# Grouped-query mixing with split values as weights, feature-major, and a written table of slots

## The reference

```python
def windowed_gqa_sink(q, k, v, sink):
...
    s = jnp.einsum('bnqhgd,bnkhd->bnhgqk', qb, kb).astype(jnp.float32) * (dh ** -0.5)
    s = jnp.where(mask[None, :, None, None], s, -jnp.inf)
...
    m = jnp.maximum(jnp.max(s, axis=-1, keepdims=True), sink_l)
    e = jnp.exp(s - m)
    p = e / (jnp.sum(e, axis=-1, keepdims=True) + jnp.exp(sink_l - m))
    o = jnp.einsum('bnhgqk,bnkhd->bnqhgd', p.astype(v.dtype), vb)

def second_block(...):
...
        merged = jax.nn.sigmoid(ga) * (ya @ w_branch_a[l]) + jax.nn.sigmoid(gb) * (yb @ w_branch_b[l])
        h = h + merged @ w_out[l]
```

## Time and profile before

| | |
|---|---|
| median of 3 runs | 960.63 us (960.3 to 960.73) |
| the profiled execution | 960.34 us, span of its instructions 958.5 us |
| granted clock | 0.998 |
| PE busy | 951.3 us, 99% |
| DVE busy | 655.8 us, 68% |
| ACT busy | 533.7 us, 56% |

### The profile page before, as it was taken

One profiled execution on the slowest core, in us unless ns is written; L12 is line 12 of the kernel. 1 busy time (PEld: TensorE's weight loads), 2 busy tenths in 40 slices (PEclk: granted clock), 3 DMA queues, 4 the chain that ended last, 5 costly groups with the idle time before them and its releaser, 6 DMA issues.

```text
span 958.5 us, 14072 instructions
## 1 busy us (share of the span) xinstructions
PE 951.3 (99%) x5478; PEld 834.8 (87%) x5478; DVE 655.8 (68%) x842; ACT 533.7 (56%) x692; POOL 57.6 (6%) x92
## 2 busy tenths in 40 slices
PE   9999999999999999999999999999999999999997
PEld 8999988888888888898888888999888898888886
DVE  6778869866665565688666566878656676566665
ACT  7577678436444444474454445678664464444544
POOL 2200000002000000022221000100000020000000
PEclk9999999999999999999999999999999999999999
DMA  9684444553755655547666555644345546665541
GB/s 308 206 255 133 132 132 159 196 181 127 266 192 188 206 175 185 187 155 247 205 214 208 180 184 166 210 141 137 130 132 176 176 167 206 200 194 180 187 160 44
DMA packets 117440, 173.17 MB, mean 181 GB/s; under 512 B 3152, under 2 KB 89440, under 8 KB 117392
## 3 DMA queue, kind: packets, MB, share of 16 engines
q1 hardware_dynamic: 115824, 168.32, 54.2%
q0 software_dynamic: 1424, 3.91, 1.4%
q10 hardware_dynamic: 144, 0.26, 0.1%
HBM read 171.44 MB, written 1.05 MB: 180 GB/s over the span
## 4 chain that ended last, share of the span: by engine, by line
PE 98%; DMA 1%; DVE 0%; SPq 0%; ACT 0%; issue 0%
PE pair L683 22%; PE pair L686 11%; PE acc L665 10%; PE acc L667 10%; PE acc L666 10%; PE pair L665 8%; PE pair L667 8%; PE pair L666 8%; PE acc L1198 1%; PE acc L1041 1%; PE pair L893 1%; PE acc L1184 1%; PE acc L810 1%; DMA raw<-in_w_in 1%; PE acc L876 1%; PE acc L729 0%
## 5 line engine op out<-in xcount | busy, mean ns | idle before, releaser
L683 PE MATMUL pair<-actp,wh 128*128 128x512 f32 x912 | 292.8, 396 | 0.0
L1735 DVE TENSOR_TENSOR wl<-raw,wh 128x2048 fp32r<-128x2048 f32 x89 | 204.9, 2303 | 62.5 <-ACT wh L1301 62.5
L1301 ACT ACTIVATE wh<-raw 128x2048 fp32r<-128x2048 f32 x88 | 168.4, 1913 | 83.5 <-PE acc L667 83.5
L686 PEld LDWEIGHTS pair<-actp,wl 128*128 128x128 f32 x912 | 171.3, 188 | 40.0
L686 PE MATMUL pair<-actp,wl 128*128 128x256 f32 x912 | 179.2, 278 | 0.0
L1730 DVE TENSOR_TENSOR wl<-raw,wh 128x2048 fp32r<-128x2048 f32 x68 | 155.4, 2288 | 31.0 <-ACT wh L1295 30.6
L1295 ACT ACTIVATE wh<-raw 128x2048 fp32r<-128x2048 f32 x69 | 132.1, 1916 | 77.4 <-PE pair L667 54.3
L683 PEld LDWEIGHTS pair<-actp,wh 128*128 128x128 f32 x912 | 141.6, 189 | 1.4
L1514 ACT ACTIVATE arena<-pair 128x512 f32<-128x512 f32 x57 | 34.1, 598 | 170.9 <-PE pair L683 170.9
L665 PE MATMUL acc<-wh,midh 128*128 128x512 f32 x310 | 120.9, 390 | 0.0
L667 PE MATMUL acc<-wh,midl 128*128 128x512 f32 x310 | 120.6, 389 | 0.0
(11 more groups left out here) (348 smaller groups left out, 1380.9 us busy)
## 6 DMA issues: line engine op xcount, KB each, us to landing
raw<-in_w_in SPq DMA_DIRECT2D x37, 1024.0 KB, 5.3
raw<-in_mlp_w SPq DMA_DIRECT2D x32, 1024.0 KB, 5.3
raw<-in_ffn_w_gate SPq DMA_DIRECT2D x22, 1024.0 KB, 5.3
raw<-in_ffn_w_up SPq DMA_DIRECT2D x22, 1024.0 KB, 5.3
raw<-in_ffn_w_down SPq DMA_DIRECT2D x22, 1024.0 KB, 5.0
raw<-in_w_out SPq DMA_DIRECT2D x8, 1024.0 KB, 5.0
raw<-in_w_up_rnn SPq DMA_DIRECT2D x4, 1024.0 KB, 5.2
raw<-in_cmp_k_w SPq DMA_DIRECT2D x2, 1024.0 KB, 5.7
```

Source lines behind the costliest of these rows:

```text
L683: return nc.tensor.matmul(bank[:, :].rearrange("p (u t) -> p u t", u=2), h[:, k, cs], actp[:, :, k, :], **kw)
L686: return nc.tensor.matmul(bank[:, 0:T], l[:, k, cs], acth[:, k, :], **kw)
L1301: nc.scalar.activation(wh[:, n % R, :], raw[:, n % R, :], ACT.Copy).then_inc(hi_ready, 1)
L1735: nc.vector.tensor_tensor(wl[:, n % R, :], raw[:, n % R, :], wh[:, n % R, :].bitcast(F32), ALU.subtract).then_inc(lo_ready, 1)
```

## The change

The neighbourhood heads keep their instructions. For the grouped-query heads (in the diff, the first `heads2` is that of ACT and the second that of DVE):

- The values become f32r weights. `vbs` holds, for each half of the keys and each group, 64 columns of the high part and 64 of the low part side by side, 128 in all. ACT copies the high part (in the round of `QB + 1`), and DVE subtracts the low part; before, one DVE copy filled `vb`.
- The probabilities are divided ahead of the transposes (`scale2`, on DVE), one slot behind the score. They alternate between two buffers, `prob2` and `prob3`.
- The transposed probabilities are split: ACT copies the high part to `pth` (`copy2`), and DVE subtracts the low part to `ptl` (`low_probs`).
- `mix2` multiplies each of the two value blocks with `pth` and `ptl`: four matmuls of 256 columns. The outcome is feature-major: partitions 0 to 63 hold the high values' product, 64 to 127 the low values'.
- ACT moves the lower rows down (`low_rows` into `ylow`), and DVE adds them (`norm2`) into `ybT`, which is feature-major. The two `turn_out` of `btok` are gone; ACT copies and DVE splits `ybT` directly.
- The table `turn2` is replaced by separate slots for score, scale, turn and mix (`SCORE_SLOTS` and the lists beside it). The turn stands two slots behind the score, and for the grouped heads the mix stands one slot behind the turn. The last mix moves from slot 31 to slot 33, right ahead of panel `BR`.

```diff
-        turn2 = {(QKV2 + 2 + k, 1): k for k in range(7)}
-        turn2[QKV2 + 9, 1] = 7
-        turn2[QKV2 + 10, 1] = 8
-        for k in range(9, 17):
-            turn2[QKV2 + 11 + (k - 9) // 2, (k - 9) % 2] = k
-        turn2[QKV2 + 15, 1] = 17
+        SCORE_SLOTS = (5, 7, 9, 11, 13, 15, 17, 19, 21, 22, 23, 25, 26, 27, 29, 30)
+        score_at = places(SCORE_SLOTS)
+        scale_at = places([at + 1 for at in SCORE_SLOTS])
+        turn_at = places((7, 9, 11, 13, 15, 17, 19, 21, 23, 24, 25, 27, 28, 29, 31, 32))
+        mix_at = places((9, 11, 13, 15, 17, 19, 21, 22, 24, 25, 26, 28, 29, 30, 32, 33))
...
             def mix2(k):
+                vt = head2(k)[3]
+                pe.wait_ge(normed, NH + k)
+                if k >= NH:
+
+                    pe.wait_ge(ptl_ready, k - NH + 1)
+                    if k == NH:
+                        pe.wait_ge(vb_ready, 1)
+                    for kt in range(TT):
+                        for pt in (pth, ptl):
+                            m = nc.tensor.matmul(ps[4][:, 0:T], vt[kt], pt[:, kt, :], start=kt == 0 and pt is pth,
+                                                 stop=kt == 1 and pt is ptl)
+                    m.then_inc(mixed, 1)
+                    return
...
-                if n == GB2 + 3:
-                    pe.wait_ge(normed, 3 * NH)
-
-                    pe.wait_ge(midl_ready, 3)
-                    for i in range(2):
-                        turn_out(OUT_B[i], btok, 2 * i)
...
+            def low_rows(k):
+
+                act.wait_ge(mixed, NH + k + 1)
+                act.wait_ge(normed, NH + k)
+                nc.scalar.activation(ylow[0:DH, :], ps[4][DH:2 * DH, 0:T], ACT.Copy).then_inc(ylow_ready, 1)
...
             def heads2(n, part):
+                if mix_at.get((n, part), 0) >= NH:
+                    low_rows(mix_at[n, part])
+                if (n, part) in turn_at:
+                    copy2(turn_at[n, part])
+                if (n, part) in score_at:
+                    exp2(score_at[n, part])
...
+            def scale2(k):
+
+                dve.wait_ge(exped, NH + k + 1)
+                o = k % 3
+                c = coef[:, o, 0:TT]
+                link(nc.vector.tensor_tensor(c, sums[:, o, 0:TT], esink[:, o, :], ALU.add))
+                link(nc.vector.reciprocal(c, c))
+                prob = prob_of(k)
+                for tt in range(TT):
+                    m = nc.vector.tensor_scalar(prob[:, tt, :], prob[:, tt, :], coef[:, o, tt:tt + 1], None, ALU.mult)
+                m.then_inc(scaled, 1)
+
+            def low_probs(k):
+
+                dve.wait_ge(probT_ready, NH + k + 1)
+                nc.vector.tensor_tensor(ptl.rearrange("p k t -> p (k t)"), ps[3][:, :],
+                                        pth.rearrange("p k t -> p (k t)").bitcast(F32), ALU.subtract).then_inc(ptl_ready, 1)
...
             def heads2(n, part):
+                if scale_at.get((n, part), 0) >= NH:
+                    scale2(scale_at[n, part])
+                if (n, part) in score_at:
+                    mask2(score_at[n, part])
+                if turn_at.get((n, part), 0) >= NH:
+                    low_probs(turn_at[n, part])
+                if (n, part) in mix_at:
+                    norm2(mix_at[n, part])
```

More of the change, by code:

```diff
@@ L194, in build @@
         kbT = carve(12288, T)
-        vb = carve(13056, TT, P)
         prob2 = carve(13312, TT, T)
         probT2 = carve(13824, 512)
+        prob3 = carve(13824, TT, T)
+        pth, ptl = mrgl[:, 4:6, :], mrgl[:, 6:8, :]
+        ylow = thr
+        vbs = midh[:, 4:6, :].rearrange("p k t -> p (k t)").rearrange("p (k g s d) -> p k g s d", k=TT, g=GR, s=2)
         atok2 = carve(14336, TT, NH * DH)
-        btok = xs[:, 0, :].rearrange("p (t n) -> p t n", t=TT)
+        ybT = xs[:, 0, :].rearrange("p (k t) -> p k t", t=T)
         vbT = xs[:, 0, 0:T]
@@ L369, in build @@
         qb_ready = sem("qb_ready")
+        vbh_ready = sem("vbh_ready")
         vb_ready = sem("vb_ready")
+        scaled = sem("scaled")
+        ptl_ready = sem("ptl_ready")
+        ylow_ready = sem("ylow_ready")
         out_ready = [sem(f"out_ready{b}") for b in range(2 * TT)]
@@ L633, in head2, with prob_of @@
             return (qst[:, h, :], mrgl[:, g, :], mrgl[:, GR + g, :],
-                    [vb[:, kt, DH * g:DH * (g + 1)] for kt in range(TT)])
+                    [vbs[:, kt, g, :, :].rearrange("p s d -> p (s d)") for kt in range(TT)])
+        def prob_of(k):
+            return prob3 if k >= NH and k % 2 else prob2
         def spread_to(j):
             return ps[TURNED[0]][:, 0:T] if j == 3 else ps[3][:, 0:T]
-        OUT_A, OUT_B = 5, (4, 5)
+        OUT_A = 5
         LOW, HIGH, LAST = (0, 1), (4, 5), (6, 7)
@@ L1202, in heads2 @@
             def heads2(n, part):
[L1203 to L1211, removed]
+                if (n, part) in mix_at:
+                    mix2(mix_at[n, part])
+                if (n, part) in turn_at:
+                    turn2_(turn_at[n, part])
+                if (n, part) in score_at:
+                    score2(score_at[n, part])
             def free_bank2(n):
@@ L1637, in _ @@
                 if n == BR:
+                    heads2(n - 1, 1)
                     done(BR - 1)
                     for i in range(2):
-                        out_hi(acth, i, OUT_B[i], 3 + i + 1)
+                        act.wait_ge(normed, 2 * NH + 4 * i + 4)
+                        nc.scalar.activation(acth[:, 2 * i:2 * i + 2, :], ybT[:, 2 * i:2 * i + 2, :], ACT.Copy).then_inc(midh_ready, 1)
                     gates2(n)
@@ L1683, in _ @@
                     swap(swk, kbT[:, :])
-                heads2(n - 1, 1)
+                if n == QB + 1:
+                    act.wait_ge(vb_turned, 1)
+                    nc.scalar.activation(vbs[:, :, :, 0, :], ps[OUT_A][:, 0:T].rearrange("p (k g d) -> p k g d", k=TT, g=GR),
+                                         ACT.Copy).then_inc(vbh_ready, 1)
+                if n != BR:
+                    heads2(n - 1, 1)
                 heads2(n, 0)
@@ L2196, in norm2 @@
                 dve.wait_ge(mixed, NH + k + 1)
                 o = k % 3
-                h = k % NH
                 c = coef[:, o, 0:TT]
[L2200 to L2205, removed]
+                link(nc.vector.reciprocal(c, sums[:, o, 0:TT]))
```

72 lines of the change are left out of this document (41 added, 31 removed).

## The result

The changed kernel takes **965.78 us** (median of 6 runs, 965.08 to 966.63) against 960.49 (960.02 to 960.73) beside it: ratio 1.0057 [1.0046, 1.0068]. The forecast was 962.9, range 960.0 to 965.3: slower, as forecast, but by more than the range held. The profiled execution takes 965.23, its span is 963.2.

What follows compares the result with a forecast made beforehand. PE was taken as the bound, 99% busy with one wait; new waits of 5.77 us less 3.5 spared gave +2.3, so 962.9 us. Its own range was 961.4 to 964.6, widened to 960.0 to 965.3.

Steps and rivals of the forecast that it cites:

- What PE was spared: On PE: cheaper mixes for eight heads and no `btok` transposes, about -3.5 us if nothing waits.
- The prediction's own two terms, 2.8 and 0.88: On PE: new mix 0.35 less a head, 2.8 for eight; eight `btok` transposes with their transition gone, 0.88.
- The division's multiply: On DVE in `scale2`, 256 columns: taken as 0.27 to the next; nearest row 0.409, estimate from the page 0.29.
- Where the waits stand: PE waits for DVE in slots 24, 25, 28, 29 and 32, summing to 5.77 us, none behind `BR`.
- the waits stay out: Rival: PE gets no waits and keeps its 3.5 us, time 957.1; 12%.
- the chains are a little shorter: Rival: each chain link 0.1 less, two long waits lose 1.4 each, -0.5 in all, 960.1; 13%.
- How long the chain is: ACT and DVE links from panel `QKV2 + 12`'s end to slot 28's mix: 688.59 to 702.51, wait 1.79.
- the clock falls: Rival: new PE waits bring half speed for one panel, 5.5 us more, 968.4; 7%.

Runs made afterwards that it cites:

- e9_gates_later: Changed kernel with panel-end `low_rows` and copy ahead of `hi`, and three rounds' gates a round later, behind the next slot's head work: 958.41 us, 0.9982.
- e6_low_first: Changed kernel with copies ahead of `hi`, gates a round later, `lo` held back in three rounds, slot 27's `low_probs` ahead of division and mask: 961.17 us, 1.0005.
- e2_gates_late: Changed kernel with only the gates of rounds 11, 13 and 15 a round later on ACT, behind the copy and exponentials: 960.66 us, 1.0003.
- after_again: The changed kernel itself, unaltered, run and traced again for the spread of its times: 966.83 us (5 runs), 1.0059.

## Why the prediction was half right

The median lies 2.9 above the forecast. About 0.9 of it is the chains, taken too short, less some saving that was taken too small; about 2.0 is the clock, which the sum had at nothing.

**What PE was spared: right.** Old instructions gone, new ones in: forecast 3.5. From slot 21 to `BR` the kernel before takes 50.59. The changed one without a fall takes 53.81, of which 6.64 are waits by the starts and 0.45 five restarts of 0.09 (a mix behind a wait takes 0.55 to 0.58 to its follower, else 0.47): 46.72 of work, 3.9 less and so a little more than forecast. `e9_gates_later` gives 48.49 - 1.40 - 0.27 = 46.82, or 3.8. The prediction's own two terms, 2.8 and 0.88, already make 3.7 and not 3.5. The mix costs 0.47 for the 0.48 forecast. Two groups of new instructions in the changed kernel (busy us, mean ns, idle before):

```profile
L1217 PE MATMUL acc<-mrgl,midh 128*128 128x256 f32 x32 | 5.5, 295 | 5.8 <-DVE mrgl L2250 4.9 <-issue 0.6 <-DVE xs L2257 0.2
...
L2244 DVE TENSOR_SCALAR arena<-arena,coef 128x256 f32<-128x256 f32 x16 | 4.9, 351 | 0.3
```

The division's multiply is 351 ns, on the line through 128 and 512 columns, and not 409. From 128 to 256 and to 512 columns it grows by 0.53 and 0.51 ns a column, and DVE's subtractions of 512 and 2048 columns (0.69 and 2.28 us) by 1.04. In this the trace agrees with the Trainium skill's doubled rate for it (VectorE: DVE Perf Modes, "The perf-mode tier table"), though not with the 0.29 that I estimated from the page.

**Where the waits stand: right.** Slots 24, 25, 28, 29 and 32, and none elsewhere from slot 21 on in this trace. From the starts they are 0.80, 0.26, 2.53, 0.34 and 2.65, plus 0.09 each: 7.0 where 5.8 was forecast (7.1 in the trace without a fall). The rivals *the waits stay out* and *the chains are a little shorter* fall.

**How long the chain is: the term that was mis-sized.** The chain to slot 28 was put at 13.9 us from the panel's end to PE. Its instructions in the changed kernel, ACT and then DVE:

```profile
688.49 1.91 ACT L1315 ACTIVATE wh<-raw 128x2048 fp32r<-128x2048 f32 x1 [2.22 <-PE pair L681]
690.43 0.38 ACT L1612 ACTIVATE thr<-acc 64x256 f32<-64x256 f32 x1
690.83 0.60 ACT L1606 ACTIVATE mrgl<-acc 128x512 fp32r<-128x512 f32 x1
...
696.69 0.48 ACT L1626 ACTIVATE esink<-small,nmax 128x1 f32<-128x1 f32 x2 [2.44 <-DVE nmax L1847]
...
698.18 0.60 ACT L1644 ACTIVATE midh<-acc 128x512 fp32r<-128x512 f32 x1
698.68 1.26 ACT L1660 ACTIVATE arena<-pair,hrstd 128x512 f32<-128x512 f32 x2
699.82 1.92 ACT L1315 ACTIVATE wh<-raw 128x2048 fp32r<-128x2048 f32 x1
701.62 0.61 ACT L1606 ACTIVATE mrgl<-acc 128x512 fp32r<-128x512 f32 x1
```

```profile
691.47 0.69 DVE L2250 TENSOR_TENSOR mrgl<-acc,mrgl 128x512 fp32r<-128x512 f32 x1 [0.38 <-ACT mrgl L1606]
692.19 0.42 DVE L2257 TENSOR_TENSOR xs<-acc,thr 64x256 f32<-64x256 f32 x1
692.64 2.29 DVE L1764 TENSOR_TENSOR wl<-raw,wh 128x2048 fp32r<-128x2048 f32 x1
694.85 0.15 DVE L2240 TENSOR_TENSOR coef<-sums,esink 128x2 f32<-128x2 f32 x1
...
695.77 0.48 DVE L1847 CUSTOM_DVE_ANT_0 arena<-acc,cst,small 128x256 f32<-128x256 f32 x1
...
702.26 0.69 DVE L2250 TENSOR_TENSOR mrgl<-acc,mrgl 128x512 fp32r<-128x512 f32 x1 [1.02 <-ACT mrgl L1606]
```

The order is the forecast's, link for link, and the length 14.6 (688.49 to 703.10). Many links were right: division 0.92 for 0.93, gates 1.14, the second `hi` 1.80. Six were taken too short. Five were put at a distance at which the next instruction starts some 0.1 us before the last one's end, as the copy at 701.62 does behind `hi` (699.82 and 1.92), and here it starts only behind that end; the sixth is the hand-over to PE. They are `hi` ahead of `low_rows` 1.94 for 1.81, `low_rows` 0.40 for 0.30, the low part ahead of the sum 0.72 for 0.61, the sum 0.45 for 0.34, the exponentials ahead of `out_hi` 1.49 for 1.37, the low part to PE 0.84 for 0.72. Together they are the 0.7 that was missing (the other links sum to what was forecast); in the second chain 0.4 were. What decides whether two instructions of an engine overlap so (both kinds wait for semaphores here) stays open, and no run tried it.

**The clock: the step that failed.** The sum took PE's matmuls at full clock behind every wait, and the rival *the clock falls* had 7% and 5.5 us, for a whole panel at half speed; the range left it out. In 10 of 12 runs it falls, once or twice by the levels of time, and takes 1.6 each time, since it is full again within some 3.5 us. Where it does not fall the kernel takes 963.4 to 963.6, inside the range in spite of the chains: it is the falls that carried the median out of it. By its own words ("its one idle stretch being 1.2 us") the prediction had no row for waits of 2.5, and nothing to hold the chance so low. Sum: 7.1 of waits less 3.9 spared is +3.2 for +2.3, or 963.5 (963.4 and 963.6 were measured where nothing falls), +1.6 for one fall gives 965.1, +3.2 for two 966.7.

## What to carry to other kernels

A change that spares the bounding engine work shortens the time that the other engines have between its hand-overs: walk the chain in program order before counting the gain, and add it up a second time with each link at its full duration, since a follower need not overlap it as it does elsewhere. Look first at what stands ahead of the hand-over for no reason (here a conversion for two panels later, and gates that nobody needs yet); moving it costs nothing, but follow the wait to its next place. An idle stretch of TensorE can have a second price, the clock behind it (here after waits of 2.4 to 2.8 us, in most runs), and a kernel whose times fall into levels should be looked at for that.

## What the runs showed of the hardware

- PE's waits of 2.4 to 2.8 us (by the starts) were followed by half clock in some executions and not in others of the same program: behind 2.65, 2.60 and 2.83 it fell, and behind 2.53, 2.59 and 2.67 it did not, nor does the length order them; in `e6_low_first` it fell behind 2.38. Waits of up to 1.53 us (`e2_gates_late`) were not followed by one: no run of it is over 0.9 us above the traced one, at full clock, where a fall takes 1.6. The Trainium skill (TensorE: Matmul & The Clock Gate, "The HAM clock gate") says that the gate runs on its own, not reset when a kernel starts, so that the same kernel meets it differently from run to run: three levels of one kernel, 963.4, 965.1 and 966.7, agree with it.
- The half clock starts at once in one case (the mix behind slot 28's wait in `after_again`, at 703.37) and 1.4 us after the work is resumed in another (722.4, slot 32 of the first trace).
- At half clock a 512-column matmul of f32r has a pitch of 0.43 us, at full 0.23.
